# Second feed-forward block: transfers between the up and down products sent in order of need, the last product and the final norm done token tile by token tile

## What is computed

```
DN_ALPHA = 2 ** 0.25;  LN_EPS = 1e-5;  D_MODEL = 1024;  D_FF_2 = 4096;  SEQ = 1024

f = jnp.square(jax.nn.relu(x @ w_up[l] + b_up[l])) @ w_down[l] + b_down[l]
x = layer_norm(DN_ALPHA * x + f, ln3_g[l], ln3_b[l])

def layer_norm(x, g, b):
    mu = jnp.mean(xf, axis=-1, keepdims=True)
    var = jnp.mean(jnp.square(xf - mu), axis=-1, keepdims=True)
    return (xf - mu) * lax.rsqrt(var + LN_EPS) * g + b
```

## Time and profile before

| | us |
|---|---|
| median of 3 runs | 3225.45 |
| lowest and highest run | 3219.58, 3229.51 |
| profiled execution, its own time | 3233.05 |
| profiled execution, its span (first to last instruction) | 3231.3 |
| down products: first and last matmul of L1784 start at | 2874.7 and 3204.8 |
| TensorE busy, share of the span | 89% |
| VectorE, ScalarE, GpSimd busy | 65%, 37%, 26% |
| mean granted TensorE clock | 0.942 |

### The profile page before, as it was taken

How to read it: one execution, slowest core, us unless ns; L and a number is a source line. 1 busy time by engine, 2 the same in 40 slices (tenths; PEclk the granted TensorE clock), 3 DMA queues, 4 the chain that set the end, 5 groups by cost and what they waited for, 6 DMA issues and landing times. The chain is left out here.

```text
span 3231.3 us, 40242 instructions
## 1 busy us (share of the span) xinstructions
PE 2872.1 (89%) x15609; PEld 2467.1 (76%) x15609; DVE 2111.8 (65%) x3136; ACT 1186.3 (37%) x1682; POOL 850.8 (26%) x336
## 2 busy tenths in 40 slices
PE   4989999799999999988668667989998899988996
PEld 3879897697888888877557665879778888867885
DVE  7627774665455555564389976874444777759998
ACT  5424444222222222223256454651321434433332
POOL 1213331113233323342031521221112222312223
PEclk9989998799999999999879878999999999999998
DMA  6733333402111111111222332131112234364432
GB/s 230 260 115 73 73 77 128 158 26 73 40 52 39 65 39 52 39 53 50 69 72 105 112 75 66 41 117 51 40 40 72 101 131 156 144 273 160 150 111 78
DMA packets 133359, 307.53 MB, mean 95 GB/s; under 512 B 55061, under 2 KB 74008, under 8 KB 116936
## 3 DMA queue, kind: packets, MB, share of 16 engines
q1 hardware_dynamic: 128167, 287.82, 26.6%
q10 hardware_dynamic: 4320, 14.29, 1.3%
q0 software_dynamic: 704, 3.15, 0.3%
HBM read 236.14 MB, written 72.23 MB: 95 GB/s over the span
## 5 line engine op out<-in xcount | busy, mean ns | idle before, releaser
L1083 PE MATMUL psum<-h_hi,w_hl 128*128 128x512 f32 x1600 | 494.7, 390 | 8.6 <-POOL w_hl L1072 5.2
L453 PE MATMUL psum<-w_hl,h_hi 128*128 128x256 f32 (+1 forms) x1920 | 355.6, 288 | 29.8 <-POOL w_hl L416 15.5
L1083 PEld LDWEIGHTS psum<-h_hi,w_hl 128*128 128x128 f32 x1600 | 300.3, 188 | 73.0 <-POOL w_hl L1072 6.0
L416 POOL TENSOR_TENSOR w_hl<-w_raw,w_hl 128x2048 fp32r<-128x2048 f32 (+2 forms) x40 | 184.3, 4608 | 565.9 <-ACT w_hl L408 565.9
L453 PEld LDWEIGHTS psum<-w_hl,h_hi 128*128 128x128 f32 x1920 | 306.8, 197 | 31.6 <-POOL w_hl L416 16.1
L1083 PE MATMUL psum<-h_lo,w_hl 128*128 128x512 f32 x800 | 311.8, 390 | 0.0
L1423 DVE TENSOR_TENSOR residual<-residual,psum 128x512 f32<-128x512 f32 x176 | 120.2, 687 | 274.9 <-PE psum L1100 274.8
L1072 POOL TENSOR_TENSOR w_hl<-w_raw,w_hl 128x2048 fp32r<-128x2048 f32 x36 | 181.0, 5027 | 441.8 <-ACT w_hl L1066 441.8
L453 PE MATMUL psum<-h_hi,w_hl 128*128 128x512 f32 (+1 forms) x864 | 256.0, 381 | 38.5 <-POOL h_lo L3348 19.0
L453 PE MATMUL psum<-w_hl,h_lo 128*128 128x256 f32 (+1 forms) x960 | 275.5, 287 | 0.0
L453 PEld LDWEIGHTS psum<-h_hi,w_hl 128*128 128x128 f32 x864 | 161.2, 193 | 69.6 <-POOL h_lo L3348 19.5
(11 more groups left out here) (447 smaller groups left out, 6641.1 us busy)
## 6 DMA issues: line engine op xcount, KB each, us to landing
w_raw<-in_w_up SPq DMA_DIRECT2D x38, 1024.0 KB, 5.0
ffn_a_raw<-ffn_operands SPq DMA_DIRECT2D x56, 512.0 KB, 3.7
ffn_operands<-ffn_ro SPq DMA_DIRECT2D x16, 1024.0 KB, 4.7
ffn_w_down<-in_w_down SPq DMA_DIRECT2D x16, 1024.0 KB, 8.5
ada_w<-in_w_ada ACTq DMA_DIRECT2D x26, 512.0 KB, 4.4
w_raw<-in_w_in_T SPq DMA_DIRECT2D x12, 1024.0 KB, 6.8
ffn_operands<-ffn_ro SPq DMA_DIRECT2D x16, 768.0 KB, 3.2
ada_w<-in_w_ada SPq DMA_DIRECT2D x22, 512.0 KB, 4.7
```

The costliest lines, as they stand in the source:

```text
L416: pool.tensor_tensor(self.k.w_lo[s][:, 0:n], self.k.w_raw[s][:, 0:n], self.k.w_hi[s][:, 0:n].bitcast(F), ALU.subtract)\
L453: mm = pe.matmul(out, lhs, rhs, start=t == 0 and p == 0, stop=t == KT - 1 and p == 2)
L1083: m = pe.matmul(k.bank[first_bank + b][:, :], w[:, t * CW + f * P:t * CW + (f + 1) * P], h[:, t, half * 512:half * 512 + 512], start=t == ...
```

## The change

Four things change, all inside `ffn_squared_relu`:

1. SyncE: `load_a` runs two halves further ahead (six before the loop, then 2q + 6 and 2q + 7). The residual comes back in four transfers that are spread out: the first after `load_a(5)`, the other three at q = 0, 1 and 2, each with a semaphore of its own (`x_back[m]`). The four `w_down` transfers of a quarter are sent one per product in steps 1 to 4 of the quarter before, not all four at step 0.
2. TensorE: the last product (q = 27) runs bank by bank, both halves of a token tile before the next tile, after it has waited for both halves' operands. All others are as before.
3. VectorE: the half statistics of tiles 0 to 3 over the left 512 columns move ahead of product 25's evacuations; the others of tiles 0 to 3, with the rest of their norm, stand ahead of product 26's. For tiles 4 to 7 the right half is taken ahead of product 27's evacuations, and then each tile is evacuated and normed before the next.
4. The norm's last two passes become one operation on VectorE (`scaled_shift`: x times 1/std plus shift). ScalarE keeps only the root, now per tile; GpSimd's pass is gone.

```
-                for u in range(4):
+                def load_x(m):
+                    sp.dma_start(k.x[:, 2 * m:2 * m + 2, :].rearrange("p a n -> p (a n)"),
+                                 x_kept[:, 2 * m * D:2 * (m + 1) * D]).then_inc(x_back[m], 16)
+                for u in range(6):
                     load_a(u)
                 sp.wait_ge(prod, nth(G - 1, 3) + 1)
-                for m in range(4):
-                    sp.dma_start(k.x[:, 2 * m:2 * m + 2, :].rearrange("p a n -> p (a n)"),
-                                 x_kept[:, 2 * m * D:2 * (m + 1) * D]).then_inc(x_back, 16)
+                load_x(0)
                 keep(G - 1)
                 for q in range(Q):
-                    if q % 7 == 0 and q // 7 + 1 < J:
-                        j = q // 7 + 1
+                    j, step = q // 7 + 1, q % 7
+                    if q < 3:
+                        load_x(q + 1)
+                    if step == 1 and j < J:
                         if j == 1:
                             sp.wait_ge(prod, 7 * (G - PLAIN))
                             sp.wait_ge(kept_a, 16 * G)
                             sp.wait_ge(kept_s, 16 * G)
...
-                        for pair in range(4 * j, 4 * j + 4):
-                            load_down(pair)
-                    for u in (2 * q + 4, 2 * q + 5):
+                    if 1 <= step < 5 and j < J:
+                        load_down(4 * j + step - 1)
+                    for u in (2 * q + 6, 2 * q + 7):
                         if u < 2 * Q:
                             load_a(u)
...
-                for q in range(Q):
+                for q in range(Q - 1):
                     for h in range(2):
-                        down(q, h)
+                        operands_ready(q, h)
+                        if q < 2 and h == 0:
+                            pe.wait_ge(dve_out, 7 * (G - 1 + q - PLAIN))
+                        for m in range(4):
+                            down(q, h, m)
+                operands_ready(Q - 1, 0)
+                operands_ready(Q - 1, 1)
+                for m in range(4):
+                    for h in range(2):
+                        down(Q - 1, h, m)
...
-                for p in range(NT // 2):
-                    act.wait_ge(aggr, 2 * p + 2)
-                    act.activation(std[:, 2 * p:2 * p + 2], mv[:, 2 * p:2 * p + 2, 1], ACT.Sqrt, bias=eps[:, 0:1])\
-                       .then_inc(std_done, 1)
-                    act.wait_ge(rstd_done, p + 1)
-                    for i in (2 * p, 2 * p + 1):
-                        act.wait_ge(gained, i + 1)
-                        act.activation(k.x[:, i, :], k.x[:, i, :], ACT.Copy, scale=rstd[:, i:i + 1]).then_inc(scaled_out, 1)
+                for i in range(NT):
+                    act.wait_ge(aggr, i + 1)
+                    act.activation(std[:, i:i + 1], mv[:, i, 1:2], ACT.Sqrt, bias=eps[:, 0:1]).then_inc(std_done, 1)
...
-                pool.wait_ge(rows_in, 32)
-                for i in range(NT):
-                    pool.wait_ge(scaled_out, i + 1)
-                    pool.tensor_tensor(k.x[:, i, :], k.x[:, i, :], srow[:, :], ALU.add).then_inc(ready, 1)
...
+                def scaled_shift(i):
+                    dve.wait_ge(std_done, i + 1)
+                    dve.reciprocal(rstd[:, i:i + 1], std[:, i:i + 1]).then_inc(rstd_done, 1)
+                    dve.wait_ge(rstd_done, i + 1)
+                    dve.wait_ge(gained, i + 1)
+                    dve.scalar_tensor_tensor(out=k.x[:, i, :], in0=k.x[:, i, :], scalar=rstd[:, i:i + 1], in1=srow[:, :],
+                                             op0=ALU.mult, op1=ALU.add).then_inc(ready, 1)
...
                     if q == Q - 2:
+                        dve.wait_ge(evac, evacuated(Q - 3, 3, 0))
                         for i in range(4):
-                            stats(i)
+                            half_stats(i, 1)
+                            moments(i)
+                            centred_gain(i)
+                            scaled_shift(i)
+                    if q == Q - 3:
+                        dve.wait_ge(evac, evacuated_whole(Q - 5, 3))
                         for i in range(4):
-                            centred_gain(i)
+                            half_stats(i, 0)
+                    if q == Q - 1:
+                        dve.wait_ge(evac, evacuated(Q - 2, 3, 0))
+                        for i in range(4, 8):
+                            half_stats(i, 1)
                     for m in range(4):
                         evacuate(q, m)
-                for i in (4, 5):
-                    stats(i)
-                centred_gain(4)
-                centred_gain(5)
-                for i in (6, 7):
-                    stats(i)
-                centred_gain(6)
-                centred_gain(7)
+                        if q == Q - 1:
+                            dve.wait_ge(evac, evacuated(q, m, 0))
+                            half_stats(m + 4, 0)
+                            moments(m + 4)
+                            centred_gain(m + 4)
+                            scaled_shift(m + 4)
```

More of the change, by code:

```diff
@@ L1605, in evacuated_whole @@
             return evacuated(q, m, len(PLACES[product(q)[0]]) - 1)
-        (bias_in, biased, scaled, x_saved, x_back, eps_made) = (
-            sem(n) for n in ("bias_in", "biased", "scaled", "x_saved", "x_back", "eps_made"))
+        (bias_in, biased, scaled, x_saved, eps_made) = (
+            sem(n) for n in ("bias_in", "biased", "scaled", "x_saved", "eps_made"))
+        x_back = [sem(f"x_back{m}") for m in range(4)]
         (s_step, s_sum, s_hi, s_lo) = (sem("s_" + n) for n in ("step", "sum", "hi", "lo"))
@@ L1617, in ffn_squared_relu @@
             sem(n) for n in ("td", "a_hi", "b_hi", "a_lo", "b_lo_dve", "b_lo_pool", "half_mm", "bank_mm", "evac", "summed"))
-        rows_in, stats_done, aggr, std_done, gained, rstd_done, scaled_out, ready, stored = (
-            sem(n) for n in ("rows_in", "stats", "aggr", "std", "gained", "rstd", "scaled_out", "ready", "stored"))
+        rows_in, stats_done, aggr, std_done, gained, rstd_done, ready, stored = (
+            sem(n) for n in ("rows_in", "stats", "aggr", "std", "gained", "rstd", "ready", "stored"))
         up_mm = wt.up_mm
@@ L1767, in _, with operands_ready @@
                         up(g, p)
[L1769 to L1773, removed]
-                    pe.wait_ge(b_lo_pool if h else b_lo_dve, q + 1)
[L1775 to L1782, removed]
-                            for n, (x_, w) in enumerate(((ah, bh), (ah, bl), (al, bh))):
-                                mm = pe.matmul(k.bank[bank_set(q) + m][:, :], x_[:, a, m * P:(m + 1) * P], w[:, a, :],
-                                               start=h == 0 and a == 0 and n == 0, stop=h == 1 and a == 1 and n == 2)
-                        if h == 1:
-                            mm.then_inc(bank_mm, 1)
-                    if h == 0:
+                def operands_ready(q, h):
+                    pe.wait_ge(a_lo, 2 * q + h + 1)
+                    pe.wait_ge(b_lo_pool if h else b_lo_dve, q + 1)
@@ new lines, in down @@
+                def down(q, h, m):
+                    ah, al, bh, bl = halves[(2 * q + h) % 4]
+                    if h == 0 and q > 1:
+                        pe.wait_ge(evac, evacuated_whole(q - 2, m))
+                    for a in range(2):
+                        for n, (x_, w) in enumerate(((ah, bh), (ah, bl), (al, bh))):
+                            mm = pe.matmul(k.bank[bank_set(q) + m][:, :], x_[:, a, m * P:(m + 1) * P], w[:, a, :],
+                                           start=h == 0 and a == 0 and n == 0, stop=h == 1 and a == 1 and n == 2)
+                    if h == 1:
+                        mm.then_inc(bank_mm, 1)
+                    elif m == 3:
@@ L2065, in add_acc, with half_stats, moments @@
                             dve.tensor_tensor(to, to, acc[:, m, :], ALU.add).then_inc(summed, 1)
-                def stats(i):
-                    dve.wait_ge(evac, tile_done(i))
-                    k.x_stats(dve, i, stats_done)
-                    dve.wait_ge(stats_done, i + 1)
+                def half_stats(i, part):
+                    dve.bn_stats(k.stats[:, i, 6 * part:6 * part + 6], k.x[:, i, H * part:H * part + H])\
+                       .then_inc(stats_done, 1)
+                def moments(i):
+                    dve.wait_ge(stats_done, 5 + i if i < 4 else 9 + i)
                     dve.bn_aggr(mv[:, i, :], k.stats[:, i, :]).then_inc(aggr, 1)
```

8 lines of the change are left out of this document (1 added, 7 removed).

## The result

| | before | after |
|---|---|---|
| median of the runs side by side, us | 3229.51 (5 runs, 3219.58 to 3233.68) | 3212.18 (5 runs, 3209.98 to 3218.41) |
| ratio after to before, 95% interval | | 0.9951 (0.9931 to 0.9972) |
| profiled execution: its own time; span | 3233.05; 3231.3 | 3218.41; 3216.6 |
| first down matmul to last down matmul (starts) | 330.07 | 311.84 |
| last down matmul (start) to the end of the span | 26.52 | 28.52 |

The kernel is 17.3 us faster by the medians, 15.8 by the ratio (0.0049 x 3229.51), 14.7 by the two spans. The two lengths in the middle say where: the front gained 18.2 us, the tail lost 2.0. Their sum is 16.2; the rest of the difference of the spans is that the stage began 1.5 us later in this execution (2876.24 against 2874.71).

The account below looks back on a forecast made before the run. TensorE sets the pace, its pauses coming from queued left-half transfers and VectorE's backlog. Front -19.0 and tail +1.4 give -17.6 us: 3215.5 from the profiled 3233.05, 3208 us from the median 3225.45; range 3201 to 3217.

Parts of the forecast that it names:

- -19.0 and +1.4: Down products: reordered transfers gain 19.0 us at the front; the rebuilt norm loses 1.4 us in the tail.
- The walk of VectorE: First down products: VectorE's operations added up by their spacings, giving product starts and a front gain of 19.0 us.
- the hold in the sums and the missing hold in the copies: Before product 2: GpSimd's piece falls into VectorE's sums, ending 2893.1 instead of 2890.9; copies, then free of it, end 2895.5.
- the pause of 1.2 us: Before product 2: TensorE free at 2896.6, VectorE's splits ready at 2897.8, so TensorE pauses 1.2 us.
- Quarter 3: Residual's last transfer, before product 4: lands at about 2911.7 behind 7.3 MB, needed at 2916, 4 us or more in hand.
- granted clock 1.0: TensorE from 2875 on: full clock throughout, since the earlier 2.64 us pause left it full and the new pauses are shorter.
- Rival 2: TensorE's clock falls in small pauses: 1.4 to 2.0 us each, four cost 7 us, gain 10.6, 3215 us; chance 0.08.
- 1.4 us pause forecast before product 7: Before product 7: TensorE free at 2956.1, VectorE's splits ready at 2957.5, so TensorE pauses 1.4 us.
- the w_down pieces: Later quarters: sending w_down one per product costs nothing, 21 us between sending and need against 8.7 us to land.
- the moved split: Tail: half statistics push the splits past GpSimd's last subtraction, so the one of 3.12 us takes 1.2.
- the tile: Tail, VectorE's norm: statistics, moments, centring, reciprocal and scaling with shift take 3.48 us per tile.
- Charging the wait: Tail, VectorE: an operation waiting on its own predecessor costs about 0.11 us; if 28 were free, 3.1 us shorter.

Follow-up runs that it names:

- e5: After, with each quarter's four w_down transfers sent together at step 1 instead of one per product: front 319.39 us, tail 28.47 (profile only).
- e2: After with SyncE's old order of transfers: front 329.08 us, tail 28.48, ratio to before 1.0008 (0.9996 to 1.002).
- e4: Before with only the left operands loaded two halves further ahead: front 317.19 us, tail 26.54, ratio to before 0.9958.
- e1: Before with only the change's order of transfers, last product and norm as before: front 311.01 us, tail 26.65, ratio to before 0.9937.
- e3: After with the last product in the old order, half by half: front 311.87 us, tail 28.50 (profile only).
- e6: After with the residual's scaling and bias cut to one column, output incomplete: front 307.45 us, tail 28.53 (profile only).
- e7: After with VectorE's norm operations ordered by kind over four tiles, last evacuations ahead of the norm: front 311.00 us, tail 24.79, ratio to before 0.9929.
- e8: e7 with tiles 0 to 3 scaled by ScalarE and shifted by GpSimd again: front 310.99 us, tail 20.02, ratio to before 0.9913.
- e9: e8 with the first two left operands sent between the second last keep's two pieces: front 314.02 us, tail 20.04, ratio to before 0.9916.

## Why the prediction was right

**The sum.** Forecast -19.0 and +1.4, measured -18.2 and +2.0: -16.2 against -17.6. The ratio's interval is 9 to 22 us of gain, and the forecast lies inside. Of the 4.2 us between 3208.0 and the median of 3212.18, 4.1 are the kernel before, whose median was 3225.45 in the runs I started from and 3229.51 in those beside the change.

**The walk of VectorE.** Its product starts, beside TensorE's of after less 1.53:

| start of product | forecast | measured |
|---|---|---|
| 2 | 2897.8 | 2897.95 |
| 3 | 2910.7 | 2910.67 |
| 4 | 2923.4 | 2923.95 |
| 5 | 2934.3 | 2936.54 |
| 7 | 2957.5 | 2958.29 |

Up to product 3 it is right to 0.15 us, the hold in the sums and the missing hold in the copies among it. That TensorE's start of product 2 agrees is in part luck: VectorE was ready as forecast (2897.71), but the pause of 1.2 us that was forecast there is filled by 1.4 us that TensorE had lost in product 0. Three things under it were not:

- *Product 4, 0.55 late.* "Quarter 3 lands at about 2911.7; it is needed at 2916." It was needed at 2914.0 (third split and two scalings after 2910.7; I had put too much ahead of it) and landed at 2914.5, 2.8 later than the volume gave. The "4 us or more in hand" were less than nothing. e5 shows what it would have meant with three more MB ahead.
- *Product 5, 2.2 late.* I had granted clock 1.0 "from 2875 on", by the one row of a 2.64 us pause that left it there. That row was no rule. The same pause of 2.62 to 2.64 us before product 0 left the clock up in four profiled executions (before, e2, e4, e5) and was followed by records at half pace in six (after, e1, e3, e6, e7, e8). Of the pauses of 2.09 to 2.18 us before product 4, three were followed by such records (after, e3, e9) and three were not (e1, e7, e8). Rival 2 thus happened in part: eight records at 0.43 instead of 0.2267 are 1.6 us at product 4, and 1.4 at product 0. The Trainium skill, page "TensorE: Matmul & The Clock Gate", section "A second HAM failure mode: psum-queue depth-cycling", has frequent small idles swing the clock. The trace agrees so far as eight records at half pace follow a pause of only 2.12 us; how frequent the pauses must be, no run here tests.
- *Product 7, only 0.8 late.* The rival's price was wrong all the same. Records at half pace delay TensorE only where it is the late one. Product 0's 1.4 us went into the 1.2 us pause that was forecast before product 2 (there is none), and 1.4 of the 2.2 us by which product 5 was late into the 1.4 us pause forecast before product 7 (none either). VectorE's backlog and the clock's loss lay beside each other; I had charged them as a sum in the rival and as nothing in the forecast. The experiments with the same order of transfers give the price: where product 4 ran at full pace the front is 311.0 (e1, e7, e8), as the forecast's 330.07 - 19.0 has it, and where it began at half pace 311.8 to 311.9 (after, e3), 0.85 us for 1.6 us of slower records.

**The causes.** That TensorE waited for left operands held up in the queue stands: undoing the order alone brings 329.08 back (e2), the earlier left operands alone give 12.9 of the 18.2 (e4). That what still stops TensorE is VectorE's backlog stands (e6). That the w_down pieces cost nothing later stands: no wait at the weight sums, median landing 5.9 us, less than in bursts. So do TensorE's bank order at nothing (e3) and the moved split (1.22 for 3.12 us).

**The tail, +2.0 for +1.4.** The start of the norm relative to the last matmul came out as forecast (13.13 us ahead of it, forecast 13.1). The mis-sized term is the tile, 3.58 for 3.48 us: the two passes of 128x1024 took 1.20 and 1.21, not the 1.17 of the row it was read from; the rest are hundredths in statistics and moments. The waits do not explain the passes, since the operation behind each does not wait for it, and in e7 they take 1.19; where the last hundredths come from was not looked into. That is 0.3 us over the first four tiles and 0.3 over the last four. Counted from the end of the last matmul the tail is 28.1 us for a forecast 27.5. Charging the wait was right, and at 0.11 rather low (0.13 in e7).

## What to carry to other kernels

When a transfer queue is in program order, look for a small transfer with an early need behind large ones with a late need, and compare the volume ahead of each with the time of its need, the last one included. Removing a stall makes the engine that was second the late one: walk it by its spacings before you price what is left, and put a clock loss into the pause that follows it rather than on top. And where operations of one engine feed each other, do them by kind over several tiles: the same instructions took 3.7 us less here, more than the whole reorganization of the tail had cost.

## What was not expected of the hardware

- The same pause of TensorE, 2.62 to 2.64 us, was followed by full clock in four executions and by six to eight records at half pace in six. TensorE's program is the same up to there in all ten, and in e5 and after, which fall on different sides, so are SyncE's transfers. No run explains it.
- GpSimd holds VectorE's operations with two SBUF inputs (a split from 1.22 to 3.41 us in e9, two scalings from 2.36 to 4.57 and a sum of 128x512 from 0.69 to 2.90 in after), but adds with one input in PSUM and half statistics run at their own pace beside it (e8).
- VectorE's moments and reciprocals, at 0.25 and 0.19 us in a chain, follow each other every 0.08 and 0.06 us when none waits for the one before (after, e7).
- The stage's first matmul starts anywhere from 2866.0 to 2882.2 us in executions that are the same up to it. Where that comes from was not looked into; it is why single executions tell nothing below some 10 us here unless the stage is measured by itself.
